# Modulation weights with output columns on partitions, one VectorE multiply-and-sum per tile, and the first projection run behind them block by block of its inner dimension

## The chip, the cores and the metric

One core of one Trainium2 chip runs the kernel. The metric is the device time of one execution in microseconds; the median of three runs of the kernel before is 2373.27 us.

## What is computed

A decoder trunk with two layers, 256 tokens and width 2048, all in float32. Cut to what matters here:

```python
mod = silu(c) @ ada_w[layer] + ada_b[layer]          # c: 2048, ada_w: 2048 x 12288, for each of 2 layers
sh1, sc1, g1, sh2, sc2, g2 = split(mod, 6)           # 2048 each
h = rms_norm(x) * (1 + sc1) + sh1
x = x + g1 * mixer(h)                                # layer 0: MoBA + differential attention, layer 1: sliding window
h = rms_norm(x) * (1 + sc2) + sh2
x = x + g2 * swiglu(h)
out = rms_norm(x) * final_norm
```

The modulation weights are 2 x 2048 x 12288 floats, 192 tiles of 1 MiB, and each is used once, for one row `c`. Nothing of layer 0's first projection can be multiplied with a token before `sc1` and `sh1` are there for the same columns.

## The kernel before

Five programs are written out by hand, one for each engine, and meet on semaphores. SyncE (SP) issues all weight transfers in one fixed order: 1 MiB tiles `raw` (128 partitions x 2048 floats, in a ring of four) for the projections and the FFN, and 1 MiB tiles `ada_raw` (a ring of two) for the modulation. `Phase` (line 62) holds the counts of each stage: `blocks` of 512 output columns, `pairs` of 128-row slices of the inner dimension, and `ada`, the 512-column modulation blocks that are worked off beside it.

Each float32 product is made of three fp32r products. ScalarE copies a weight pair to `w_hi` (`hi`, line 425), VectorE subtracts it from the raw weights to get `w_lo` (`lo`, line 674), four pairs deep, and TensorE runs 12 matmuls of 128x512 on each pair (`pair`, line 1156: lines 1164 to 1166). There are 728 pairs.

**Modulation.** A tile holds inner dimension on partitions and 4 x 512 output columns. `ada_product` (line 694) multiplies a 512-column slice by a per-partition scalar of `cond` and adds it to `acc`: 16 instructions for 512 columns, 4 for each tile, lines 697 and 699. What stands in `acc` is still to be summed over the 128 partitions: TensorE transposes it (`sums`, line 1170: 8 transposes for half a vector, 24 such halves), VectorE reduces the transposed block (`columns`, line 722: line 727), and adds the bias (line 731).

**Start.** `mod0` works off the first eight 512-column blocks (shift and scale of layer 0, 32 tiles). The norm of `x`, its transposes (`norm_blocks`, line 1187), the modulation of the transposed blocks (line 456 on ScalarE, 768 on VectorE) and then the first projection follow.

**First projection.** `ab(0)` to `ab(3)` each make three 512-column blocks (q, k, v of four heads), 24 pairs each, with output column block outermost and inner dimension innermost; in the PE program of `ab(i)` the attention of unit i-1 is interleaved. `ab_rope` (line 803) rotates q and k on VectorE, `ab_v` and `copy_kT` (lines 815, 819) copy on VectorE, and two modulation blocks (8 tiles, 32 products) go beside each `ab(i)`. The output projection (`AB_OUT`, 32 pairs) carries 16 tiles. After it come norm 1 (`to_norm`), the FFN, norm 2, layer 1, norm 3, the second FFN and the last norm.

## Time and profile before

| | |
|---|---|
| median of 3 runs | 2373.27 us (2373.07 to 2379.73) |
| profiled execution, its own time | 2372.14 us |
| its span in the trace | 2370.2 us |
| TensorE busy | 2195.5 us, 93% |
| VectorE busy | 1743.5 us, 74% |
| ScalarE busy | 955.9 us, 40% |
| DMA | 593.12 MB, mean 250 GB/s |

The busy shares are sums over the whole span and say little of a stage; a stage is read from windows cut at the starts of its pairs. TensorE records are pipelined, so that one of 390 ns starts every 227 ns: the distance of the starts is the cost.

### The profile page before, as it was taken

What the parts mean: (1) busy time and instruction counts of PE and PEld (TensorE: products, weight loads), DVE (VectorE), ACT (ScalarE), POOL (GpSimd) and SP (SyncE); (2) the same over time, 40 slices, a digit from 0 to 9 for tenths busy, and PEclk for the clock granted to TensorE, in tenths of its full rate; (3) what the DMA queues carried; (4) which work ended last, traced back from release to release, by engine and by line L of the source; (5) the groups of instructions that cost most, each with busy time, mean ns of one, the idle gap of its engine ahead of it and who ended that gap; (6) DMA issues with size and microseconds to landing.
All of it is one profiled execution on the core that took longest, in us unless ns stands there. A gap on an engine that the chain in (4) does not pass through costs nothing.

```text
span 2370.2 us, 27802 instructions
## 1 busy us (share of the span) xinstructions
PE 2195.5 (93%) x10348; PEld 1831.9 (77%) x10348; DVE 1743.5 (74%) x2089; ACT 955.9 (40%) x1236; POOL 10.2 (0%) x23
## 2 busy tenths in 40 slices
PE   0199999999999999999998999898999999999997
PEld 0178888777888888888886788787888888888886
DVE  6898889998779977798777856498776545455554
ACT  1054434435443344434444344344443344434443
POOL 0000000000000000000000000000000000000000
PEclk9699999999999999999999999899999999999998
DMA  8876776786777977789766633285774555555543
GB/s 337 341 299 271 288 299 234 290 330 256 284 282 296 382 288 289 270 356 357 283 245 252 240 113 111 90 329 214 291 282 176 191 185 194 191 188 191 194 153 149
DMA packets 82437, 593.12 MB, mean 250 GB/s; under 512 B 9408, under 2 KB 9440, under 8 KB 10784
## 3 DMA queue, kind: packets, MB, share of 16 engines
q1 hardware_dynamic: 81056, 587.25, 64.5%
q0 software_dynamic: 1280, 4.51, 0.7%
q8 instruction: 66, 1.08, 0.2%
q14 instruction: 35, 0.29, 0.0%
HBM read 589.62 MB, written 2.10 MB: 250 GB/s over the span
## 4 chain that ended last, share of the span: by engine, by line
PE 49%; issue 35%; DVE 9%; DMA 3%; ACT 1%; DVEq 1%; SPq 0%; POOL 0%; ACTq 0%; POOLq 0%
PE ps L1164 14%; PE ps L1166 14%; PE ps L1165 14%; DVE acc L699 4%; DMA ada_raw<-in_ada 3%; PE ps L1153 2%; DVE w_lo L677 2%; PE ps L1231 1%; PE ps L1236 1%; PE ps L1234 0%; PE ps L1248 0%; PE ps L1251 0%; PE ps L1250 0%; ACT gate L493 0%; DVEq L971 0%
## 5 line engine op out<-in xcount | busy, mean ns | idle before, releaser
L677 DVE TENSOR_TENSOR w_lo<-raw,w_hi 128x1024 fp32r<-128x1024 f32 x728 | 888.7, 1223 | 421.1 <-ACT w_hi L431 417.9
L431 ACT ACTIVATE w_hi<-raw 128x1024 fp32r<-128x1024 f32 x728 | 767.7, 1061 | 1059.4 <-PE ps L1166 958.0
L1164 PE MATMUL ps<-w_hi,xT_hi 128*128 128x512 f32 x1952 | 769.2, 394 | 15.7 <-DVE w_lo L677 7.7
L1166 PE MATMUL ps<-w_hi,xT_lo 128*128 128x512 f32 x1952 | 761.3, 390 | 0.0
L1165 PE MATMUL ps<-w_lo,xT_hi 128*128 128x512 f32 x1952 | 760.3, 390 | 0.0
L699 DVE SCALAR_TENSOR_TENSOR acc<-ada_raw,cond,acc 128x512 f32<-128x512 f32 (+1 forms) x656 | 486.1, 747 | 17.3 <-DMA ada_raw<-in_ada 9.9
L1164 PEld LDWEIGHTS ps<-w_hi,xT_hi 128*128 128x128 f32 x1952 | 367.0, 188 | 93.3 <-issue 14.2
L1166 PEld LDWEIGHTS ps<-w_hi,xT_lo 128*128 128x128 f32 x1952 | 366.7, 188 | 77.4
L1165 PEld LDWEIGHTS ps<-w_lo,xT_hi 128*128 128x128 f32 x1952 | 367.2, 188 | 73.8
L1164 PE MATMUL ps<-w_hi,hT_hi 128*128 128x512 f32 x960 | 377.4, 393 | 3.4 <-DVE hT_lo L896 1.9
L1166 PE MATMUL ps<-w_hi,hT_lo 128*128 128x512 f32 x960 | 374.4, 390 | 0.0
L1165 PE MATMUL ps<-w_lo,hT_hi 128*128 128x512 f32 x960 | 374.2, 390 | 0.0
L1164 PEld LDWEIGHTS ps<-w_hi,hT_hi 128*128 128x128 f32 x960 | 180.7, 188 | 41.8 <-DVE w_lo L677 2.3
L1166 PEld LDWEIGHTS ps<-w_hi,hT_lo 128*128 128x128 f32 x960 | 180.6, 188 | 38.0
L1165 PEld LDWEIGHTS ps<-w_lo,hT_hi 128*128 128x128 f32 x960 | 180.8, 188 | 36.6
L1153 PE MATMUL ps<-ident,work 128*128 128x128 f32 x448 | 71.3, 306 | 47.2 <-ACT work L535 26.3
L1153 PEld LDWEIGHTS ps<-ident,work 128*128 128x128 f32 x448 | 62.9, 161 | 56.3 <-ACT work L535 26.5
L1153 PE MATMUL ps<-ident,acc 128*128 128x128 f32 x192 | 27.3, 296 | 82.7 <-DVE acc L699 82.7
L1153 PEld LDWEIGHTS ps<-ident,acc 128*128 128x128 f32 x192 | 25.0, 154 | 85.3 <-issue 64.5
L1012 DVE TENSOR_TENSOR hT_lo<-ps,hT_hi 128x512 f32 (+1 forms) x44 | 30.4, 692 | 71.3 <-ACT hT_hi L593 71.3
L593 ACT ACTIVATE hT_hi<-ps 128x512 f32 (+1 forms) x44 | 26.4, 599 | 96.4 <-PE ps L1153 96.4
L699 DVE SCALAR_TENSOR_TENSOR acc<-raw,cond,acc 128x512 f32<-128x512 f32 (+1 forms) x64 | 43.1, 746 | 3.1 <-DMA raw<-in_ada 3.0
(145 smaller groups left out, 915.7 us busy)
## 6 DMA issues: line engine op xcount, KB each, us to landing
ada_raw<-in_ada SPq DMA_DIRECT2D x176, 1024.0 KB, 6.2
raw<-in_ffn_in SPq DMA_DIRECT2D x176, 1024.0 KB, 4.8
raw<-in_ffn_out SPq DMA_DIRECT2D x88, 1024.0 KB, 6.6
...
```

The costliest lines, as they stand in the source:

```text
L431: nc.scalar.activation(w_hi[:, p % PAIRS, :, :], raw[:, t % RAW, 2 * (p % 2):2 * (p % 2) + 2, :], ACT.Copy).then_inc(hi_ready, 1)
L593: nc.scalar.activation(hT_hi[:, ds(2 * j, 2), :], bank(4 + b).rearrange("p (k s) -> p k s", k=2), ACT.Copy).then_inc(hTh_done, 1)
L677: tt(w_lo[:, p % PAIRS, :, :], raw[:, (p // 2) % RAW, 2 * (p % 2):2 * (p % 2) + 2, :], w_hi[:, p % PAIRS, :, :].bitcast(F32), ALU.subtract ...
L699: stt(out=dst, in0=src, scalar=cond[:, kt:kt + 1], in1=dst, op0=ALU.mult, op1=ALU.add).then_inc(ada_step, 1)
L1012: tt(hT_lo[:, ds(2 * j, 2), :], bank(4 + b).rearrange("p (k s) -> p k s", k=2), hT_hi[:, ds(2 * j, 2), :].bitcast(F32), ALU.subtract).then ...
L1153: return nc.tensor.transpose(out, in_, ident[:, :])
L1164: mm(out, hi[:, kt, tok], w_hi[:, q % PAIRS, k, :], start=(kt == 0), stop=False)
L1165: mm(out, hi[:, kt, tok], w_lo[:, q % PAIRS, k, :], start=False, stop=False)
L1166: last = mm(out, lo[:, kt, tok], w_hi[:, q % PAIRS, k, :], start=False, stop=(kt == 2 * ph.pairs - 1))
L1231: mm(s0, q(h)[:, 0:P], k(h)[:, 0:P], start=False, stop=True)
L1236: last = mm(ps[:, s1 + P:s1 + SEQ], q(h)[:, P:SEQ], k(h)[:, P:SEQ], start=False, stop=True)
```

## The change

The tiles of the modulation weights are laid out the other way round: a tile is 128 output columns on the partitions and all 2048 inner rows along them. `cond` becomes a row of 2048 on every partition, and one VectorE instruction (`tile`) multiplies a tile by it and writes the sum to one column of `mod`. The products, the partial sums `acc`, the 24 x 8 transposes and the reductions are gone; only the bias is added (`with_bias`). The tiles at the start alternate between scale and shift for the same 128 columns and use four slots (`ada_raw` twice, `spare`, `gate`).

With this, two 128-column slices of the modulated input are known after each four tiles. A new phase `AB0` holds the first unit's three blocks, and in eight rounds each round takes four tiles, the bias, the two slices, and one pair of each of the three blocks, that is, with the inner dimension outermost. Three pairs of banks hold the three sums. The rotations of the first unit follow the eighth round, its transposes stand inside `ab(1)`, and the attention of unit 0 is five pairs later there (`AB_LATER`). The copies of v and of the transposed k move from VectorE to ScalarE; k is rotated into a place of its own (`nat_k`). Each `ab(i)` for i = 1, 2, 3 now carries 12 tiles and `AB_OUT` 12.

```diff
+        self.block0 = prev.block0 + prev.n * prev.evacs if prev else 0
         self.ada0 = prev.ada0 + prev.n * prev.ada if prev else 0
         self.fills = [len(range(s, self.quads, RAW)) for s in range(RAW)]
         self.fills0 = [a + prev.n * b for a, b in zip(prev.fills0, prev.fills)] if prev else [0] * RAW
@@ -83,9 +83,9 @@
...
-
-
-
-FFN_SUMS = (((None, G2[0]), (SH1[1], SC1[1]), (G1[1], None)), ((None, G2[1]), (None, None), (None, None)))
...
+            sp.dma_start(cond[:, :], T["c"].partition_broadcast(P)).then_inc(s_cond, 16)
+            for t in range(TT):
+                sp.dma_start(x[:, t, :], T["x"][:, t, :]).then_inc(x_landed[t], 16)
+            def start_tile(m):
+                if m >= START_SLOTS:
+                    sp.wait_ge(ada_done, ADA_CREDIT + m - START_SLOTS + 1)
+                sp.dma_start(ada_slot[m % START_SLOTS], T["ada"][m]).then_inc(ada_landed[m % START_SLOTS], 16)
+
+            def weights(ph, i, t):
+                sp.wait_ge(lo_ready, LO_CREDIT + 2 * (ph.quad(i, t) - ph.raw_distance(t) + 1))
+                sp.dma_start(raw[:, t % RAW, :, :].rearrange("p a n -> p (a n)"),
+                             T[ph.src][ph.src0 + i * ph.quads + t]).then_inc(raw_landed[t % RAW], 16)
+            for j in range(8):
+                for m in range(4 * j, 4 * j + 4):
+                    start_tile(m)
+                for t in range((3 * j + 1) // 2, (3 * j + 4) // 2):
+                    if t == 3:
+                        sp.wait_ge(s_setup, 1)
+                    weights(AB0, 0, t)
+            for n, ph in enumerate(chain):
...
+            def copy_kT(u):
+                act.wait_ge(kT_done, u + 1)
+                nc.scalar.activation(kT, bank(6, 2).rearrange("p (h s) -> p h s", h=4), ACT.Copy).then_inc(kT_copied, 1)
+
+            def copy_v(u):
+                act.wait_ge(pair_used, AB_IN.used(u - 1, 2) if u else AB_IN.used(-1, 2))
+                nc.scalar.activation(v_ab, bank(2 * (u % 2) if u else 4, 2).rearrange("p (t n) -> p t n", t=TT),
+                                     ACT.Copy).then_inc(v_copied, 1)
...
+            for j in range(8):
+                act.wait_ge(mods_ready, j + 1)
+                act.wait_ge(x0T_done, j + 1)
+                for k in range(2):
+                    kt = 2 * j + k
+                    o = ps[:, (6 + j % 2) * 512 + k * SEQ:(6 + j % 2) * 512 + (k + 1) * SEQ]
+                    last = nc.scalar.activation(o, o, ACT.Identity, bias=mod[:, 0, 0, kt:kt + 1],
+                                                scale=mod[:, 0, 1, kt:kt + 1])
+                last.then_inc(x0m_done, 1)
+                act.wait_ge(x0m_done, j + 1)
+                nc.scalar.activation(xT_hi[:, 2 * j:2 * j + 2, :], bank(6 + j % 2).rearrange("p (k s) -> p k s", k=2),
+                                     ACT.Copy).then_inc(x0h_done, 1)
+                for n in range(3 * j, 3 * j + 3):
+                    hi(AB0, 0, n)
+            copy_v(0)
+            act.wait_ge(s_setup, 1)
+            nc.scalar.activation(lam[:, 2:4], lam[:, 0:2], ACT.Exp).then_inc(lam_exp, 1)
...
+            def tile(slot, q):
+                nc.vector.scalar_tensor_tensor(
+                    out=ada_slot[slot], in0=ada_slot[slot], scalar=1.0, in1=cond[:, :], op0=ALU.mult, op1=ALU.mult,
+                    accum_out=mod_row[:, ds(q, 1)]).then_inc(ada_done, 1)
+
+            def ada(ph, i, a):
+
+                dve.wait_ge(ada_landed[a % ADA_RAW], 16 * ph.ada_fills(i, a))
+                tile(a % ADA_RAW, ph.ada_tile(i, a))
+
+            def start_tile(m):
+
+                dve.wait_ge(ada_landed[m % START_SLOTS], 16 * (m // START_SLOTS + 1))
+                tile(m % START_SLOTS, (1 - m % 2) * KT + m // 2)
 
             def ada_behind(ph, i, p):
 
-                for step in ph.ada_steps(p):
-                    ada(ph, i, step)
...
+            nc.vector.tensor_copy(mask_prev[:, :], masks[:, 128:256])
+            for layer in range(2):
+                scales = ada_bias[:, layer, 1:5:3, :]
+                nc.vector.tensor_scalar(scales, scales, 1.0, None, ALU.add)
+            lv = lam_rows.rearrange("p (a b n) -> p a b n", a=2, b=2)
+            prod = raw[:, 3, 2, 0:256].rearrange("p (a n) -> p a n", a=2)
             tt(prod, lv[:, :, 0, :], lv[:, :, 1, :], ALU.mult)
             dve.drain()
-            nc.vector.tensor_reduce(lam[:, 0:2], prod, AX_X, ALU.add).then_inc(s_setup, 2)
-            dve.wait_ge(s_setup, 5)
-            tt(lam[:, 0:1], lam[:, 3:4], lam[:, 2:3], ALU.subtract)
+            nc.vector.tensor_reduce(lam[:, 0:2], prod, AX_X, ALU.add).then_inc(s_setup, 1)
+            dve.wait_ge(x_landed[1], 16)
+            stt(out=squared[:, 1, :], in0=x[:, 1, :], scalar=1.0, in1=x[:, 1, :], op0=ALU.mult, op1=ALU.mult,
+                accum_out=squares[:, 1, 0:1])
             dve.drain()
-            nc.vector.tensor_scalar(lam[:, 0:1], lam[:, 0:1], -LAMBDA_INIT, None, ALU.add).then_inc(s_setup, 1)
-            repeat(dve, 1, 3, mod0)
-            columns(SH1[0], 0, 6, order=0)
-            columns(SC1[0], 0, 4, order=1)
             norm(0)
-            mod0(3)
-            columns(SH1[0], 1, 6, order=2)
-            columns(SC1[0], 1, 4, order=3)
-            norm_out(0, AB_IN)
+            dve.wait_ge(s_silu_c, 1)
+            for j in range(8):
+                for m in range(4 * j, 4 * j + 4):
+                    start_tile(m)
+                dve.drain()
+                pair_mods = mod[:, 0, 0:2, 2 * j:2 * j + 2]
+                tt(pair_mods, pair_mods, ada_bias[:, 0, 0:2, 2 * j:2 * j + 2], ALU.add).then_inc(mods_ready, 1)
+                lo(AB0, 0, 3 * j)
+                dve.wait_ge(x0h_done, j + 1)
+                tt(xT_lo[:, 2 * j:2 * j + 2, :], bank(6 + j % 2).rearrange("p (k s) -> p k s", k=2),
+                   xT_hi[:, 2 * j:2 * j + 2, :].bitcast(F32), ALU.subtract).then_inc(x0l_done, 1)
+                lo(AB0, 0, 3 * j + 1)
+                lo(AB0, 0, 3 * j + 2)
 
             def ab_stage(stage, u, kind):
 
                 B = kind == "B"
-                if stage == "v":
...
+            ab_rope(0, 0)
+            ab_rope(0, 1)
             ab(1, "A")
...
@@ -1167,20 +1173,9 @@
                                   stop=(kt == 2 * ph.pairs - 1))
                 last.then_inc(pair_used, 1)
 
-            def sums(n, h, b=6, steps=None, read=None):
-
-
-                slot0 = 4 * n % ACC + 2 * h
-                pe.wait_ge(ada_step, ADA_CREDIT + (16 * (4 * n + 2 * h + 2) if steps is None else steps))
-                pe.wait_ge(acc_free, ACC_CREDIT + (4 * n + 2 * h if read is None else read))
-                for c in range(8):
-                    last = tr(ps[:, b * 512 + c * P:b * 512 + (c + 1) * P],
...
+            def first_blocks(j):
+
+                pe.wait_ge(xn_done, j // 2 + 1)
+                if j >= 2:
+                    pe.wait_ge(x0l_done, j - 1)
+                for k in range(2):
+                    kt, at = 2 * j + k, (6 + j % 2) * 512 + k * SEQ
+                    for t in range(TT):
+                        last = tr(ps[:, at + t * P:at + (t + 1) * P], xn[:, t, kt * P:(kt + 1) * P])
+                last.then_inc(x0T_done, 1)
 
             def q_transposes(i):
 
...
-            norm_blocks(0, (2, 3))
+            first_blocks(0)
+            first_blocks(1)
+            for j in range(8):
+                pe.wait_ge(x0l_done, j + 1)
+                for b in range(3):
+                    pair(AB0, 0, b, j, AB0_SLOT[b], xT_hi, xT_lo, q=3 * j + b)
+                if j < 6:
+                    first_blocks(j + 2)
+            pe.wait_ge(s_setup, 1)
 
...
```

**The order on VectorE at the start.** In the program before, behind the loop with the rest of the 32 tiles, this is the last part of the modulation and what stands between it and the first weights (`acc` partial sums, `mod` the vectors, `ps` the banks):

```order
L699 SCALAR_TENSOR_TENSOR acc<-raw,cond,acc 128x512 [waits ada_step,raw_landed3,raw_landed2]
L699 SCALAR_TENSOR_TENSOR acc<-raw,cond,acc 128x512 [waits ada_step] x7
L727 TENSOR_REDUCE mod<-ps 128x8 [waits mods_summed]
L731 SCALAR_TENSOR_TENSOR mod<-mod,ada_bias 128x16
L727 TENSOR_REDUCE mod<-ps 128x8 [waits mods_summed]
L731 SCALAR_TENSOR_TENSOR mod<-mod,ada_bias 128x16
L768 TENSOR_SCALAR ps<-ps,mod 128x256 [waits xT_done]
L768 TENSOR_SCALAR ps<-ps,mod 128x256
L768 TENSOR_SCALAR ps<-ps,mod 128x256 [waits xT_done]
L768 TENSOR_SCALAR ps<-ps,mod 128x256
L773 TENSOR_TENSOR xT_lo<-ps,xT_hi 128x1024 [waits xT_hi_done]
L677 TENSOR_TENSOR w_lo<-raw,w_hi 128x1024 [waits hi_ready] x2
```

And in the changed program, the end of the setup and the first of eight rounds:

```order
L762 RECIPROCAL rstd<-rstd 128x2 [waits root_done]
L722 SCALAR_TENSOR_TENSOR ada_raw,mod<-ada_raw,cond 128x2048 [waits ada_landed0,silu_c_done]
L722 SCALAR_TENSOR_TENSOR ada_raw,mod<-ada_raw,cond 128x2048 [waits ada_landed1]
L722 SCALAR_TENSOR_TENSOR spare,mod<-spare,cond 128x2048 [waits ada_landed2]
L722 SCALAR_TENSOR_TENSOR gate,mod<-gate,cond 128x2048 [waits ada_landed3]
L927 TENSOR_TENSOR mod<-mod,ada_bias 128x2x2
L718 TENSOR_TENSOR w_lo<-raw,w_hi 128x1024 [waits hi_ready]
L930 TENSOR_TENSOR xT_lo<-ps,xT_hi 128x512 [waits first_xT_hi_done]
L718 TENSOR_TENSOR w_lo<-raw,w_hi 128x1024 [waits hi_ready] x2
L722 SCALAR_TENSOR_TENSOR ada_raw,mod<-ada_raw,cond 128x2048 [waits ada_landed0]
```

All products stood ahead of the first `w_lo` before; now four tiles stand ahead of three of them, and the first `w_lo` of a round waits for ScalarE, which follows behind the bias (L927).

**The order on ScalarE at the start.** Before, all blocks of `x` are modulated (`ps`) and copied (`xT_hi`) once, around the first four weight pairs (L431):

```order
L535 ACTIVATE work<-x,rstd 128x512 [waits rstd_done]
L535 ACTIVATE work<-x,rstd 128x512 x7
L456 ACTIVATE ps<-ps,mod 128x256 [waits xT_done,acc_free]
L456 ACTIVATE ps<-ps,mod 128x256
L456 ACTIVATE ps<-ps,mod 128x256 [waits xT_done]
L456 ACTIVATE ps<-ps,mod 128x256
L463 ACTIVATE xT_hi<-ps 128x1024 [waits modulated_dve,modulated_act]
L431 ACTIVATE w_hi<-raw 128x1024 [waits pair_used,raw_landed0]
L431 ACTIVATE w_hi<-raw 128x1024 [waits pair_used]
L456 ACTIVATE ps<-ps,mod 128x256 [waits xT_done]
L456 ACTIVATE ps<-ps,mod 128x256
```

In the changed program the first round and the head of the second:

```order
L553 ACTIVATE work<-x,rstd 128x512 x7
L563 ACTIVATE ps<-ps,mod 128x256 [waits first_xT_done,mods_ready]
L563 ACTIVATE ps<-ps,mod 128x256
L567 ACTIVATE xT_hi<-ps 128x512 [waits first_xT_modulated]
L444 ACTIVATE w_hi<-raw 128x1024 [waits pair_used,raw_landed0]
L444 ACTIVATE w_hi<-raw 128x1024 [waits pair_used]
L444 ACTIVATE w_hi<-raw 128x1024 [waits pair_used,raw_landed1]
L563 ACTIVATE ps<-ps,mod 128x256 [waits first_xT_done,mods_ready]
L563 ACTIVATE ps<-ps,mod 128x256
```

What was one passage of ScalarE is now eight, each behind the bias of its round, and the first `w_hi` of a round stands behind the round's `xT_hi`.

## Rows read from the trace of the kernel before

**Rows 1.** Page, busy time and share of the span by engine

```profile
PE 2195.5 (93%) x10348; PEld 1831.9 (77%) x10348; DVE 1743.5 (74%) x2089; ACT 955.9 (40%) x1236; POOL 10.2 (0%) x23
```

**Rows 2.** Windows by stage: busy us by engine, TensorE clock, DMA share, GB/s

```profile
0.00:126.70 126.70, 14.47 (x65) 13.09 (x65) 95.03 (x151) 19.79 (x39) 4.79 (x13) 0.80 0.85 340
126.70:196.70 70.00, 67.65 (x306) 55.90 (x307) 67.51 (x85) 30.94 (x33) 0.00 (x0) 1.00 0.74 292
196.70:272.40 75.70, 75.70 (x381) 63.75 (x380) 65.30 (x84) 32.42 (x46) 0.00 (x0) 1.00 0.71 278
...
424.90:530.00 105.10, 100.87 (x490) 83.76 (x489) 99.22 (x127) 44.67 (x72) 0.00 (x0) 1.00 0.78 311
...
544.40:1284.00 739.60, 739.20 (x3348) 612.38 (x3348) 604.11 (x684) 305.73 (x324) 0.00 (x0) 1.00 0.77 298
```

**Rows 3.** Timeline, end of the start: start us, us, engine, line, count, idle before

```profile
110.64 5.38 DVE L699 SCALAR_TENSOR_TENSOR acc<-raw,cond,acc 128x512 f32<-128x512 f32 x8
...
116.07 3.67 PE L1153 MATMUL ps<-ident,acc 128*128 128x128 f32 x16 [18.20 <-DVE acc L699]
...
121.08 0.17 DVE L731 SCALAR_TENSOR_TENSOR mod<-mod,ada_bias 128x16 f32<-128x16 f32 x1
...
126.68 0.47 PE L1164 MATMUL ps<-w_hi,xT_hi 128*128 128x512 f32 x1 [1.69 <-DVE w_lo L677]
```

**Rows 4.** Windows of 10 us in the start

```profile
20.00:30.00 10.00, 0.00 (x0) 0.00 (x0) 8.54 (x13) 0.00 (x0) 0.00 (x0) 1.00 1.01 419
110.00:120.00 10.00, 3.67 (x16) 3.27 (x16) 7.63 (x13) 0.00 (x0) 0.00 (x0) 0.50 0.96 387
```

**Rows 5.** Timeline of the start, setup and norm 0

```profile
36.89 0.42 DVE L910 TENSOR_REDUCE lam<-work 128x2 f32<-128x256 f32 x1
...
91.94 0.15 DVE L744 TENSOR_REDUCE ssq<-squares 128x2 f32<-128x8 f32 x1
...
92.61 0.17 DVE L750 RECIPROCAL rstd<-rstd 128x2 f32<-128x2 f32 x1 [0.27 <-ACT rstd L446]
```

**Rows 6.** DMA issues of the start: engine, count, KB, median us to landing

```profile
work<-in_lam POOLq DMA_DIRECT2D x1, 256.0 KB, 13.0
```

**Rows 7.** Groups by line: operands, count | busy us, mean ns | idle before, releasers

```profile
L677 DVE TENSOR_TENSOR w_lo<-raw,w_hi 128x1024 fp32r<-128x1024 f32 x728 | 888.7, 1223 | 421.1 <-ACT w_hi L431 417.9
...
L431 ACT ACTIVATE w_hi<-raw 128x1024 fp32r<-128x1024 f32 x728 | 767.7, 1061 | 1059.4 <-PE ps L1166 958.0 <-DMA raw<-in_ffn_out 47.3 <-DMA raw<-in_swa_in 21.3
...
L699 DVE SCALAR_TENSOR_TENSOR acc<-ada_raw,cond,acc 128x512 f32<-128x512 f32 (+1 forms) x656 | 486.1, 747 | 17.3 <-DMA ada_raw<-in_ada 9.9
...
L456 ACT ACTIVATE ps<-ps,mod 128x256 f32<-128x256 f32 x32 | 16.0, 548 | 36.7 <-DVE mod L731 23.5 <-PE ps L1153 13.2
...
L439 ACT ACTIVATION_READ_ACCUMULATOR xT_lo<-x 128x1 f32 x40 | 7.4, 186 | 0.0
...
L1144 DVE SCALAR_TENSOR_TENSOR work<-x,rstd,gate 128x1024 f32<-128x1024 f32 x4 | 4.9, 1278 | 2.0 <-DMA gate<-in_final_norm 2.0
```

**Rows 8.** Timeline of TensorE in the fourth unit of the first projection

```profile
406.51 1.03 PE L1153 MATMUL ps<-ident,acc 128*128 128x128 f32 x8
407.30 0.48 PE L1164 MATMUL ps<-w_hi,xT_hi 128*128 128x512 f32 x1
...
408.08 0.39 PE L1164 MATMUL ps<-w_hi,xT_hi 128*128 128x512 f32 x1
...
408.76 0.39 PE L1164 MATMUL ps<-w_hi,xT_hi 128*128 128x512 f32 x1
```

**Rows 9.** Timeline of VectorE, one rotation in the second unit

```profile
251.93 0.42 DVE L796 TENSOR_TENSOR gate<-ps,rope_ab 128x256 f32<-128x256 f32 x1
...
256.37 0.75 DVE L699 SCALAR_TENSOR_TENSOR acc<-ada_raw,cond,acc 128x512 f32<-128x512 f32 x1
```

**Rows 10.** Timeline of VectorE and ScalarE in norm 1

```profile
535.94 0.16 DVE L750 RECIPROCAL rstd<-rstd 128x2 f32<-128x2 f32 x1
...
534.67 0.20 ACT L446 ACTIVATE rstd<-ssq 128x2 f32<-128x2 f32 x1 [0.47 <-DVE ssq L746]
```

354 lines of the change are left out of this document (138 added, 216 removed).

## The prediction

> **What bounds the kernel now.** I read the busy times first, then windows by stage, then the timeline at the seams. TensorE is busy for 93% of the span and VectorE for 74% [rows 1]. By stage: nothing of the trunk is multiplied in the first 126.7 us; TensorE's 14.5 us there are transposes. From there each of the four units of the first projection takes 70.0 to 76.8 us with TensorE busy without a gap from the second on [rows 2] (the third has the second's times, the window between them is left out). So the kernel has two parts: a start of 126.7 us on VectorE and DMA, and a rest that TensorE sets. The seam shows the start's chain: last products at 110.6, transposes of `acc` at 116.1, bias at 121.1, first matmul at 126.7 [rows 3]. TensorE's own prices: three matmuls from 408.08 to 408.76, so 0.227 us each and 2.72 for a pair of 12; eight transposes from 406.51 to 407.30, 0.79 us [rows 8].
>
> **The tile.** Eight products of 512 take 5.38 us, 0.67 each [rows 3]. The same kind of instruction, two float32 operands in SBUF and a scalar, has 1278 ns for 1024 elements [rows 7] where one of 512 has 747 (the page's mean for L699), 1.037 ns an element. A tile of 2048 is then 0.67 + 1536 x 1.037 ns = 2.27 us. Its sum output is in no VectorE row. Nearest rows: none (0), or ScalarE's reading of its accumulator, 0.19 us [rows 7]. I take 0.1, nearer to the middle since only a read is added: **2.37 us a tile**, against 4 x 0.67 = 2.7 before.
>
> **A round of the new start**, on VectorE: four tiles 9.5; drain and bias, small operations as in norm 1, 0.35; then it waits for ScalarE, which modulates two slices (2 x 0.55, overlapped: 1.0), copies 512 columns to `xT_hi` (half of `w_hi`'s 1.06, with its fixed part 0.6) and makes the round's first `w_hi` (1.06) [rows 7], 2.75 with the hand-overs; three `w_lo` at 1.14 (starts of one 1223 ns row behind another) and `xT_lo` 0.6: 4.0. Sum **16.6 us**. What lies beside it: transfers of four tiles and one and a half weight tiles, 5.5 MiB = 5.77 MB. At the 419 GB/s of a full stretch [rows 4] that is 13.8 us, hidden; SP refills a tile slot as soon as its tile is summed, 14 us ahead. TensorE has three pairs and four transposes: 8.6 us at full clock, 17.2 at half, since 16 transposes take 3.67 us at the end of the start [rows 3], where the clock is 0.50 [rows 4], against 1.6 at full. It is idle for some 8 us a round, so I expect both levels in each round.
>
> **When the rounds start.** The constants stand first in VectorE's queue: issue at 5.7, landing 13.0 later [rows 6], 18.7. That landing was already beside a full queue of tiles; `cond` as a broadcast row (1 MiB more) and `x` (2 MiB) stand ahead of the tiles now, so that the tiles, not the constants, come later. Casts and lambda, 2 us (L910 was the last of them [rows 5]), the squares of half of `x`, 2.3 as a tile, and the norm, 0.9 [rows 5], follow: first tile at **24.5 us**. The eighth round's last `xT` slice is ready at 24.5 + 7 x 16.6 + 14.4 = 155.1. TensorE's next pair, at half clock, ends at 160.5; the two rotations, 4.4 each [rows 9], and the first `w_lo` of unit 1 follow in VectorE's queue: 170.6. TensorE has finished its three pairs by about 167 and waits. I add 2.0 for a clock that fell in the gap: unit 1 begins at **172.6**, against 196.7 before: **-24.1**.
>
> **Behind the start.** Unit 1 also has the transposes of q and k of unit 0: 2 x 0.79, **+1.6**. VectorE's load in a unit: 65.3 [rows 2], less 32 products (21.1) and two copies (2.3), plus 12 tiles (28.4): 70.3 of TensorE's 75.7. I tallied both queues pair by pair: VectorE stays one to nine us ahead, least behind the second rotation. In unit 1 the two late rotations make 79.5 against 77.3, but the attention comes five pairs later. I put **0** for stalls; the cover is a lead of only 1 us at one place, and its loss is a rival below. ScalarE takes the copies, at 32.4 of 75.7 [rows 2]. The partial sums' transposes: 24 halves, four in the start, six in the three norms, where TensorE waits for VectorE anyway, and 14 in full stretches: 14 x 0.79 = **-11.1**. In norm 1 the reduction started at 534.55 and the reciprocal at 535.94, while ScalarE's root was ready at 534.87 [rows 10]: 0.85 goes; in the other two norms the root comes 1.3 later behind a table load, 0.2 each: **-1.2**. The output projection has 105.1 - 100.9 = 4.2 us of gaps with VectorE busy for 99.2 [rows 2]; 64 products (42.7) become 12 tiles (28.4): I take half the gaps, **-2.0**. Its bounds are 0 and 4.2. In the FFN nothing waits for products: 0, covered by 135 us of idle VectorE in the first one's 740. Bytes are the same.
>
> Sum: -24.1 + 1.6 - 11.1 - 1.2 - 2.0 = **-36.8 us**. From the profiled execution's 2372.1 that gives 2335.3; its own time is 1.1 under the median, from which I count: 2373.3 - 36.8 = **2336.5**.
>
> **Rule against row.** The products L699 read two float32 tensors from SBUF at 1.037 ns an element and write one, with no sum output. The Trainium skill (Vector Engine (DVE) Microarchitecture Reference, "Points that are easy to get wrong") says of this instruction that with two non-bf16 SBUF sources it runs at half throughput, because no read port is left for the accumulator. The rows contradict it for the form without a sum, and no run here shows the form with one. By the rule the kernel would be the first rival.
>
> **Rivals.**
> - *The sum halves the tile's rate*: 2048 x 1.037 = 2.1 us more a tile, 4.4 in all. For: the accumulator is new here. Against: the same operands stream at full rate. The rounds take 25.1 us and unit 1 begins 68 us later, +44 against before; each unit's VectorE load is 95 to 104 where TensorE needs 76, together +66; the output projection +4, the first FFN (84 tiles, VectorE from 604 to 747 of 740) +20. With the -12 of transposes and norms: **2495**, slower. It decides from 0.7 us more a tile: 32 x 0.7 = 22 in the rounds, 3 x (12 x 0.7 - 4.7) = 11 in the units, which uses up the gain. 10%.
> - *VectorE binds in the units*: its 5 us of slack are not where the two rotations stand, and TensorE waits 3 to 4 us in each of three. For: the lead of 1 us. Against: the tally. **2347**. 17%.
> - *TensorE stays at half clock through the rounds*: 17.2 > 16.6 sets the round, +5, and the tail of three pairs and the head of unit 1 cost 5 more. For: 0.50 in the start and 8 us idle a round. Against: bursts of three pairs are longer than the transposes that stayed cold [rows 3]. **2346**. 12%. The Trainium skill (TensorE: Matmul & The Clock Gate, "Loop structure matters more than you think") warns of this loop nest, a wait in front of every K step; by it the clock falls in every round.
> - *Transfers set the round*: 5.77 MB at the start's mean 340 GB/s [rows 2] is 17.0; at the 3.35 us a tile of the old start (32 tiles in 107 us) it is 18.4, +14: **2351**. Against: there the slots were refilled in groups, here singly. 8%.
> - *The start gains nothing*, since constants, norm and rotations only move: only the transposes and norms remain, **2361**. The order speaks against it. 3%.
>
> **Numbers.** Forecast 50%, 2336.5. Its own bounds: no cost of the sum (-3), clock never late (-5), all gaps (-2) give 2326; a sum of 0.19 (+3) and 3 us of stalls 2343. With the second to fourth rivals the range is 2324 to 2358, which leaves out the first and the last and a little more. A difference under 0.3% (7 us) can't be told from none here: faster 0.88, same 0.02, slower 0.10.
>
> **What would show it.** Right: tiles near 2.4 us, 16.6 us from a round's first tile to the next's, first tile at 24 to 25, unit 1 beginning near 172, units of 75 to 77 us, no TensorE gaps in them above 1 us. Wrong: tiles above 3 us; VectorE idle before tiles for DMA; TensorE waiting for `w_lo` in units 1 to 3.

## The result and the profile after

The changed kernel takes **2331.45 us** (median of 4 runs, 2328.86 to 2332.46) against 2374.66 us for the kernel before (4 runs, 2373.07 to 2379.73): ratio **0.9818, 95% interval 0.9805 to 0.9832**. The forecast was 2336.5, -36.8 us; the measured difference is -43.2. The profiled spans are 2329.6 and 2370.2 us, -40.6, and the account below is made between these two.

A "pair" is 12 matmuls of one pair of weight slices, as before. Its lines are now L1170 to L1172, `w_hi` is L444, `w_lo` L718, the tile L722, the bias L927.

The times of the table, and those of pairs below, lie up to 0.3 us behind the start of the matmul's own row in the timeline (unit 1: 163.5 here, 163.24 there), in all kernels alike.

| first matmul of | before | after | difference | gained in the stage |
|---|---|---|---|---|
| unit 1 | 196.7 | 163.5 | -33.2 | -33.2 |
| unit 2 | 272.4 | 245.3 | -27.1 | +6.1 |
| unit 3 | 348.1 | 321.0 | -27.1 | 0.0 |
| output projection | 424.9 | 400.1 | -24.8 | +2.3 |
| first feed-forward | 544.4 | 517.9 | -26.5 | -1.8 |
| end of span | 2370.2 | 2329.6 | -40.6 | -14.1 |

Page of the kernel after, busy time and share of the span by engine, to be held against [rows 1]: VectorE has 120 us less to do, TensorE 4 us less.

```profile
PE 2191.1 (94%) x10156; PEld 1821.1 (78%) x10156; DVE 1623.3 (70%) x1676; ACT 964.1 (41%) x1247; POOL 9.9 (0%) x22
```

Windows by stage, kernel after (window, length, then busy us of PE, PEld, DVE, ACT, POOL, TensorE clock, DMA share, GB/s), against [rows 2]: the start, units 1 to 3, the output projection, the first feed-forward layer.

```profile
0.00:163.50 163.50, 89.86 (x321) 70.78 (x322) 118.91 (x135) 52.77 (x74) 4.57 (x12) 0.88 0.87 341
...
163.50:245.30 81.80, 80.65 (x398) 67.45 (x397) 72.08 (x79) 34.05 (x49) 0.00 (x0) 0.96 0.77 298
245.30:321.00 75.70, 75.70 (x381) 63.72 (x380) 66.52 (x72) 30.75 (x44) 0.00 (x0) 1.00 0.83 322
321.00:400.10 79.10, 75.43 (x363) 62.43 (x362) 68.06 (x87) 34.74 (x56) 0.00 (x0) 1.00 0.82 324
400.10:504.60 104.50, 100.36 (x474) 83.21 (x472) 82.82 (x87) 48.00 (x75) 0.00 (x0) 0.98 0.75 301
517.90:1250.00 732.10, 732.10 (x3288) 606.34 (x3286) 561.24 (x507) 308.38 (x326) 0.00 (x0) 1.00 0.78 304
```

Timeline of VectorE, kernel after, one round of the start (start us, us, engine, line, operation, tiles, count, idle before).

```profile
71.22 2.28 DVE L722 SCALAR_TENSOR_TENSOR ada_raw<-ada_raw,cond 128x2048 f32<-128x2048 f32 x1
73.44 0.08 DVE L722 DVE_READ_ACCUMULATOR ada_raw<-ada_raw,cond 128x1 f32 x1
73.44 2.28 DVE L722 SCALAR_TENSOR_TENSOR ada_raw<-ada_raw,cond 128x2048 f32<-128x2048 f32 x1
...
80.25 0.16 DVE L927 TENSOR_TENSOR mod<-mod,ada_bias 128x4 f32<-128x4 f32 x1
83.04 1.23 DVE L718 TENSOR_TENSOR w_lo<-raw,w_hi 128x1024 fp32r<-128x1024 f32 x1 [2.63 <-ACT w_hi L444]
84.19 0.68 DVE L930 TENSOR_TENSOR xT_lo<-ps,xT_hi 128x512 fp32r<-128x512 f32 x1
84.79 2.35 DVE L718 TENSOR_TENSOR w_lo<-raw,w_hi 128x1024 fp32r<-128x1024 f32 x2
87.06 2.28 DVE L722 SCALAR_TENSOR_TENSOR ada_raw<-ada_raw,cond 128x2048 f32<-128x2048 f32 x1
```

Three things are to be seen. A tile starts every 2.21 us, and the reading of its sum (0.08 us) starts with the next tile and lies beside it: it costs nothing of its own. The round from tile to tile is 87.06 - 71.22 = **15.84 us**. And 2.63 us of it VectorE is idle for `w_hi`. The round three later, on ScalarE, says why: ScalarE stood idle 11.37 us for the bias, and its three `w_hi` come only then, behind the modulation and `xT_hi`.

```profile
127.94 0.99 ACT L563 ACTIVATE ps<-ps,mod 128x256 f32<-128x256 f32 x2 [11.37 <-DVE mod L927]
128.96 0.60 ACT L567 ACTIVATE xT_hi<-ps 128x512 fp32r<-128x512 f32 x1
129.45 2.94 ACT L444 ACTIVATE w_hi<-raw 128x1024 fp32r<-128x1024 f32 x3
```

Timeline of VectorE at the end of the start, kernel after: the last bias and slice, the first instructions of the two rotations, the first `w_lo` of unit 1.

```profile
143.57 0.17 DVE L927 TENSOR_TENSOR mod<-mod,ada_bias 128x4 f32<-128x4 f32 x1
...
147.51 0.68 DVE L930 TENSOR_TENSOR xT_lo<-ps,xT_hi 128x512 fp32r<-128x512 f32 x1
...
152.89 0.42 DVE L805 TENSOR_TENSOR gate<-ps,rope_ab 128x256 f32<-128x256 f32 x1 [2.43 <-PE ps L1172]
...
157.34 0.42 DVE L805 TENSOR_TENSOR gate<-ps,rope_ab 128x256 f32<-128x256 f32 x1
...
161.87 2.36 DVE L718 TENSOR_TENSOR w_lo<-raw,w_hi 128x1024 fp32r<-128x1024 f32 x2 [0.21 <-ACT w_hi L444]
```

Three places where TensorE waited, at the head of unit 1 and in unit 3 (timeline of TensorE, kernel after): the first is that `w_lo` behind the rotations; the other two were not forecast.

```profile
163.24 0.76 PE L1170 MATMUL ps<-w_hi,xT_hi 128*128 128x512 f32 x1 [4.93 <-DVE w_lo L718]
```

```profile
340.21 0.87 PE L1159 MATMUL ps<-ident,gate 128*128 128x128 f32 x6 [2.04 <-DVE gate L863]
364.44 1.09 PE L1159 MATMUL ps<-ident,work 128*128 128x128 f32 x8 [1.63 <-DVE work L885]
```

The waits in unit 3, kernel after: ScalarE's for weights, and the transfer queue's, 321 to 400 us (engine and line, what it waited for, us in total, times, longest).

```profile
ACT w_hi L444 <- DMA raw<-in_ab_in: 23.7, 7, 5.0
```

```profile
SPq L362 <- DVE ada_raw L722: 63.1, 12, 12.7
```

**Where the last 14.1 us are.** I compared the distances of all 728 pairs' first matmuls, kernel by kernel. Behind the first feed-forward matmul, exactly ten pairs come 0.79 or 0.80 us sooner behind the one ahead, at 698.3, 706.9, 800.3, 819.8, 966.9, 975.5, 1065.3, 1084.8, 1761.4 and 1770.1 us: the ten halves of transposes that stood there, 7.9 us. Two seams behind norms give 0.5 and 0.6. The pairs about norm 2 (1266 to 1303 us) give 3.5 net, the first of them 2.8. The last 1.6 us are steps below 0.3 us each.

### The profile page after: what moved, and what is told of

The parts are those of the page before. It is cut to its first block, busy times and chain, and to the rows that moved or that the text cites. A ratio compares the mean times of both kernels' runs of the same rounds, so it can differ in the third digit from the quotient of the medians.

```text
span 2329.6 us, 26534 instructions
## 1 busy us (share of the span) xinstructions
PE 2191.1 (94%) x10156; PEld 1821.1 (78%) x10156; DVE 1623.3 (70%) x1676; ACT 964.1 (41%) x1247; POOL 9.9 (0%) x22
## 4 chain that ended last, share of the span: by engine, by line
PE 51%; issue 35%; DVE 9%; ACT 3%; DMA 2%; DVEq 1%; POOL 0%; SPq 0%; ACTq 0%; POOLq 0%
PE ps L1170 15%; PE ps L1172 15%; PE ps L1171 15%; DVE w_lo L718 3%; DVE ada_raw L722 2%; PE ps L1159 2%; ACT w_hi L444 1%; DVE spare L722 1%; DVE gate L722 1%; ACT gate L512 1%; DMA raw<-in_lam 1%; DMA raw<-in_swa_in 1%; PE ps L1227 0%; PE ps L1232 0%; PE ps L1180 0%
## 5 line engine op out<-in xcount | busy, mean ns | idle before, releaser
L718 DVE TENSOR_TENSOR w_lo<-raw,w_hi 128x1024 fp32r<-128x1024 f32 x728 | 882.9, 1223 | 518.5 <-ACT w_hi L444 513.8
L444 ACT ACTIVATE w_hi<-raw 128x1024 fp32r<-128x1024 f32 x728 | 766.0, 1061 | 1003.6 <-PE ps L1172 866.9
L1170 PE MATMUL ps<-w_hi,xT_hi 128*128 128x512 f32 x1952 | 778.7, 399 | 57.8 <-DVE xT_lo L930 43.6
L1172 PE MATMUL ps<-w_hi,xT_lo 128*128 128x512 f32 x1952 | 768.8, 394 | 0.0
L1171 PE MATMUL ps<-w_lo,xT_hi 128*128 128x512 f32 x1952 | 768.7, 394 | 0.0
L1170 PEld LDWEIGHTS ps<-w_hi,xT_hi 128*128 128x128 f32 x1952 | 372.1, 191 | 138.4 <-DVE xT_lo L930 45.9
L1172 PEld LDWEIGHTS ps<-w_hi,xT_lo 128*128 128x128 f32 x1952 | 371.7, 190 | 79.8
L1171 PEld LDWEIGHTS ps<-w_lo,xT_hi 128*128 128x128 f32 x1952 | 372.6, 191 | 75.6
L722 DVE SCALAR_TENSOR_TENSOR ada_raw<-ada_raw,cond 128x2048 f32<-128x2048 f32 x176 | 401.1, 2283 | 2.9 <-DMA ada_raw<-in_ada 1.9
L1170 PE MATMUL ps<-w_hi,hT_hi 128*128 128x512 f32 x960 | 376.4, 392 | 2.1 <-DVE hT_lo L899 1.9
L1172 PE MATMUL ps<-w_hi,hT_lo 128*128 128x512 f32 x960 | 374.2, 390 | 0.0
L1170 PEld LDWEIGHTS ps<-w_hi,hT_hi 128*128 128x128 f32 x960 | 180.8, 188 | 39.7 <-DVE hT_lo L899 2.2
L1172 PEld LDWEIGHTS ps<-w_hi,hT_lo 128*128 128x128 f32 x960 | 180.6, 188 | 38.0
L1159 PEld LDWEIGHTS ps<-ident,work 128*128 128x128 f32 x448 | 59.7, 154 | 58.5 <-issue 40.6
L563 ACT ACTIVATE ps<-ps,mod 128x256 f32<-128x256 f32 x16 | 7.9, 533 | 84.0 <-DVE mod L927 84.0
L980 DVE TENSOR_TENSOR work<-ps,gate 128x1024 f32<-128x1024 f32 x28 | 34.1, 1219 | 12.3 <-PE ps L1172 11.7
L983 DVE TENSOR_TENSOR x<-x,work 128x1024 f32<-128x1024 f32 x32 | 39.2, 1225 | 2.4
```

The source lines that it names most:

```text
L444: nc.scalar.activation(w_hi[:, p % PAIRS, :, :], raw[:, t % RAW, 2 * (p % 2):2 * (p % 2) + 2, :], ACT.Copy).then_inc(hi_ready, 1)
L718: tt(w_lo[:, p % PAIRS, :, :], raw[:, (p // 2) % RAW, 2 * (p % 2):2 * (p % 2) + 2, :], w_hi[:, p % PAIRS, :, :].bitcast(F32), ALU.subtract ...
L722: nc.vector.scalar_tensor_tensor(out=ada_slot[slot], in0=ada_slot[slot], scalar=1.0, in1=cond[:, :], op0=ALU.mult, op1=ALU.mult, accum_out ...
L980: tt(upd, src, gate[:, ds(j * NT, NT)].unsqueeze(1).broadcast_to([P, TT, NT]), ALU.mult)
L983: tt(xs, xs, upd, ALU.add).then_inc(evacuated, 1)
L1159: return nc.tensor.transpose(out, in_, ident[:, :])
```

## The experiments

All are edits of the changed kernel. Each ran beside the kernel before; the ratio is to that one. The changed kernel itself is at 0.9818 (0.9805 to 0.9832), 2331.45 us.

**1. The tiles ahead of the rounds.** All 32 tiles first, then the eight rounds. In the transfer queue the first four blocks of weights go behind the fifth to eighth group of four tiles, the other eight behind all tiles.

```
-            for j in range(8):
-                for m in range(4 * j, 4 * j + 4):
-                    start_tile(m)
+            for m in range(START_TILES):
+                start_tile(m)
+            for j in range(8):
                 dve.drain()
```

> All 32 multiplies of the start come ahead of the eight rounds; the rounds' products, k-outermost, are unchanged. If the gain of the start is the overlap of products with tiles (the prediction's own account), the tiles end at about 32 x 2.5 = 80 us behind 21, at about 103 us, since the transfers alone set them there, and 24 pairs at 2.72 us, the slices of xT and the rotations follow: unit 1 begins at about 174 us instead of 163.5, and the time is about 2342 us, some 11 us over the changed kernel. If the gain of the start is merely that sums and transposes left TensorE, the order is worth nothing: 2331 us.

Measured: **2358.75 us**, ratio 0.9936 (0.9917 to 0.9955); unit 1 begins at 189.6. The windows of its start, up to its first pair and from there:

```profile
0.00:114.00 114.00, 2.16 (x9) 1.79 (x10) 79.50 (x81) 16.68 (x26) 4.59 (x12) 1.00 0.91 368
114.00:189.60 75.60, 70.68 (x313) 57.98 (x314) 42.27 (x55) 37.78 (x48) 0.00 (x0) 0.98 0.50 181
```

The overlap of products with tiles is worth 27 us, much more than the 11 I expected: the tiles took 2.67 us each, held by their transfers (first bias at 109.1 instead of 103), and the rounds, bound by TensorE, 8.65 us each (pair distances 3.08, 2.84, 2.72) where I had put 8.16, without the round's four transposes. So of the 33 us the start gained, 26 are the order; only 7 remain if the same work stands in the old order (189.6 against 196.7).

**2. The first `w_hi` of each round ahead of the modulation.**

```
             for j in range(8):
+                hi(AB0, 0, 3 * j)
                 act.wait_ge(mods_ready, j + 1)
...
-                for n in range(3 * j, 3 * j + 3):
+                for n in range(3 * j + 1, 3 * j + 3):
```

> ScalarE makes the first w_hi of a round before it waits for that round's modulation. If the VectorE chain sets the round (four tiles, three w_lo, one xT_lo, and 2.63 us in which VectorE waits for this very w_hi), the period falls from 15.83 us by up to 2.6 us until the transfers bind at 5.77 MB / 419 GB/s = 13.8 us: 8 x 2.0 = 16 us less, about 2315 us. If the transfers or TensorE set the round already, the period stays at 15.8 us and the time at 2331 us.

Measured: **2315.86 us**, ratio 0.9754 (0.9735 to 0.9772), 15.6 us less. The round in VectorE's timeline has lost the wait:

```profile
103.54 0.16 DVE L928 TENSOR_TENSOR mod<-mod,ada_bias 128x4 f32<-128x4 f32 x1
103.62 1.22 DVE L719 TENSOR_TENSOR w_lo<-raw,w_hi 128x1024 fp32r<-128x1024 f32 x1
105.39 0.69 DVE L931 TENSOR_TENSOR xT_lo<-ps,xT_hi 128x512 fp32r<-128x512 f32 x1 [0.55 <-ACT xT_hi L568]
```

The distance from round to round falls from 15.83 to 14.1 us in all rounds, since VectorE's 2.63 us of waiting have become 0.80 (0.55 for `xT_hi`, 0.25 for `w_hi`), and unit 1 begins 13.9 us sooner, at 149.6; the rest lies behind. The transfers run at 402 GB/s with a share of 0.98, and TensorE's clock is 0.88 (window 36 to 135 us): VectorE's chain did set the rounds of the changed kernel, neither the transfers nor TensorE.

```profile
36.00:135.00 99.00, 73.57 (x278) 58.22 (x278) 92.70 (x92) 31.65 (x43) 0.00 (x0) 0.88 0.98 402
```

At 14.1 us it is still VectorE's chain: from 50 to 135 us VectorE waits for ScalarE only (3.3 and 1.8 us in all), never for a tile to land. With a share of 0.98 the transfers leave little room behind it; how much wasn't tried.

**3. Halves of unit 1 ahead of the second rotation.**

```
             ab_rope(0, 0)
+            lo(AB_IN, 0, 0)
+            lo(AB_IN, 0, 1)
             ab_rope(0, 1)
```

and the same on ScalarE, ahead of the copy of v.

> The halves of the first two pairs of unit 1 are made ahead of the second rotation and of the copy of v, instead of behind them. If TensorE waits there for w_lo behind the rotation (w_lo 161.87, rotation 157.34 to 161.8), unit 1 begins about 4.3 us earlier, and TensorE, less cold, loses less at its head; some of it is given back if the transposes of k then wait for the second rotation: 2326 to 2328 us. If the start is set by what is behind (transfers of unit 1), the time stays at 2331 us.

Measured: **2329.49 us**, ratio 0.981 (0.9791 to 0.9828). Unit 1 begins 4.8 us sooner, at 158.7, but then TensorE waits for the third pair's `w_lo`:

```profile
158.44 0.47 PE L1176 MATMUL ps<-w_hi,xT_hi 128*128 128x512 f32 x1 [0.40 <-DVE w_lo L721]
167.28 0.50 PE L1176 MATMUL ps<-w_hi,xT_hi 128*128 128x512 f32 x1 [2.24 <-DVE w_lo L721]
```

and the half clock comes behind it (0.67 over the next 5.2 us). The first feed-forward matmul is 4.3 us sooner (513.6), yet the median falls by 2 only, which the interval doesn't separate from nothing. In the trace 3.4 us are lost again at two pairs of layer 1's attention, which is experiment 8's matter.

**4. TensorE kept at work in the rounds.** A product with a matrix of zeros is added to an open sum 18 times behind rounds 0 to 6.

```
+                    for _ in range(FILL):
+                        mm(bank(2)[:, 0:P], zeros[:, :], ident[:, :], start=False, stop=False)
```

> TensorE adds a zero product to an open sum 18 times behind rounds 0 to 6, in the time in which it would idle; numbers don't change. If the pairs that ran at half clock (4.44 us instead of 2.72 in the last round, 5.26 us at the head of unit 1) cost the end of the start, the time falls by 1.7 to 4 us, to about 2328 us. If the half clock only lengthened pairs that had time to spare, it stays at 2331 us; and if the filler delays the slices of xT, it rises by up to 0.5 us a round, to 2335 us.

Measured: **2328.73 us**, ratio 0.9808 (0.979 to 0.9826). Windows from 38 to 150 us, the changed kernel and this one:

```profile
38.00:150.00 112.00, 78.79 (x281) 62.05 (x280) 92.91 (x93) 30.97 (x42) 0.00 (x0) 0.84 0.91 360
```

```profile
38.00:150.00 112.00, 98.60 (x534) 84.58 (x534) 92.92 (x93) 30.96 (x42) 0.00 (x0) 0.95 0.91 359
```

The clock rises from 0.84 to 0.95 (the first pair of a round, 4.4 to 5.3 us in all eight rounds before, takes 2.9 in three of them) and the rounds stay at 15.83 us: the half clock had time to spare there. Unit 1 begins at 163.6. The 2.7 us of the medians aren't separated from nothing by the intervals; in the trace 1.0 lies at the first pair of unit 1 (4.21 instead of 5.26 us), 0.7 in unit 3 and 1.6 net at two pairs of the output projection.

The last round is another matter, and this experiment doesn't reach it, although zero products stand ahead of it: its first pair takes 4.44 us in both kernels, and the first rotation, whose sum that pair completes, waits for it. In the combinations of experiment 9 that pair takes 2.9 us. VectorE's wait for it, here and in the last combination:

```profile
153.00 0.42 DVE L807 TENSOR_TENSOR gate<-ps,rope_ab 128x256 f32<-128x256 f32 x1 [2.43 <-PE ps L1175]
```

```profile
137.24 0.42 DVE L824 TENSOR_TENSOR gate<-ps,rope_ab 128x256 f32<-128x256 f32 x1 [0.54 <-PE ps L1195]
```

In experiment 2, whose rounds are as short as the combination's, the wait is 2.04: the half clock costs the end of the start about 1.5 us, and nothing in the rounds before.

**5. A slower tile.**

```
             def tile(slot, q):
+                part = ada_slot[slot][:, 0:640]
+                tt(part, part, part, ALU.max)
+                dve.drain()
```

> Every tile of modulation weights gets a second VectorE instruction of 640 columns (the maximum of a piece with itself, nothing changes) and a drain, some 0.75 us a tile. If VectorE's tiles set the start as said, it lengthens by 32 x 0.75 = 24 us; in the units 12 x 0.75 = 9 us go on VectorE's 66.5 to 72 us of 76 to 82 us, so 0 to 5 us a unit: some 2331 + 24 + 0 to 15 = 2355 to 2370 us, which is the rival of a slow summing tile at the point where it was said to decide (2361 to 2370). If the transfers or TensorE set the start, 2331 to 2340 us.

Measured: **2391.38 us**, ratio 1.0072 (1.0054 to 1.0089): 60 us over the changed kernel, and slower than the kernel before. The added instruction takes 818 ns, with its drain 0.9 us a tile. Units 2 and 3:

```profile
276.60:358.50 81.90, 77.81 (x382) 64.69 (x381) 78.47 (x87) 32.21 (x47) 0.00 (x0) 0.98 0.81 314
358.50:445.00 86.50, 78.91 (x364) 64.98 (x363) 78.04 (x98) 34.23 (x56) 0.00 (x0) 0.96 0.75 291
```

The start lengthened by 29.2 us (32 x 0.91), the units by 2.1, 6.2 and 7.4, the output projection by 1.0. The rest, behind the first feed-forward matmul, took 14.5 us more, where I expected none: 8.7 of them are in five pairs in the middle of the first feed-forward layer, where TensorE waited for `w_lo`, two of them here.

```profile
801.43 0.50 PE L1173 MATMUL ps<-w_hi,hT_hi 128*128 128x512 f32 x1 [0.71 <-DVE w_lo L718]
825.40 0.50 PE L1173 MATMUL ps<-w_hi,hT_hi 128*128 128x512 f32 x1 [1.87 <-DVE w_lo L718]
```

VectorE's idle time there is an average; these waits suggest that its lead is short where a tile, the copies of a hidden block and a `w_lo` stand together.

**6. Ten groups of eight transposes back** in the feed-forward layers, at their old places.

```
+                            if (layer, s) in ((0, 0), (0, 1), (1, 0)) and p in (0, 3):
+                                eight()
```

and the same two in the input blocks of the other groups.

> The ten groups of eight transposes that the change removed from the feed-forward stretches stand again at their ten places, of the identity into a bank that nobody reads. If TensorE sets those stretches, each costs the 0.79 us by which the pair behind it moved: 7.9 us, 2339.3 us. If something else set them, under 2 us.

Measured: **2342.66 us**, ratio 0.9851 (0.9826 to 0.9877). The ten pairs come 0.78 to 0.81 us later, each, as expected. The time is 11.2 us up and not 7.9: in the profiled run another 2.6 us are at two pairs of layer 1's attention (at 1487 and 1492 us), which the edit doesn't touch. One of the four runs took 2333.38 us, at a mean clock of 0.980 where the other three had 0.977. The reading rests on the ten distances, not on the time.

**7. Tiles asked for later.** In the three units the transfer queue asks for each tile two blocks of weights later.

```
+                            late += [(ph, i, a) for a in ph.ada_after(t)]
+                            while len(late) > LAG:
+                                ada(*late.pop(0))
```

> In the three units the transfer queue asks for each tile of modulation weights two blocks of projection weights later than now, so that a wait for a free tile buffer (63.1 us in 12 waits in unit 3) holds up the weights less. If that order makes the weights late in unit 3 (ScalarE waits 4.95 and 4.19 us for them, TensorE 2.2 us), the 2.2 us and perhaps some of the norm's start come back: 2327 to 2329 us. If the bandwidth is the limit (0.82 busy), 2331 us; if now VectorE waits for its tiles, up to 2335 us.

Measured: **2330.94 us**, ratio 0.9814 (0.9797 to 0.983): nothing in the time. But unit 3 falls from 79.1 to 77.0 us, and ScalarE's wait for this unit's weights, 23.7 us in 7 places, is gone. (Unit 1 falls from 81.8 to 80.4, at its first two pairs, 4.26 us for 5.26 and 3.51 for 3.91, as in experiment 4: that is the clock.) The queue's waits in unit 3 are now split between tiles and weights:

```profile
SPq L363 <- DVE ada_raw L734: 41.2, 11, 8.6
SPq L372 <- DVE w_lo L730: 24.1, 8, 8.3
```

Of the two gaps in unit 3, the one at 340.2 us (2.04) is gone: it came from the order of the queue. With two buffers for tiles and four for weights, a tile that waits for its buffer holds up weights that have theirs. The gap at 364.4 (1.63) stands as it was, though ScalarE no longer waits for weights ahead of it:

```profile
361.73 1.09 PE L1171 MATMUL ps<-ident,work 128*128 128x128 f32 x8 [1.64 <-DVE work L897]
```

It is VectorE's: a rotation, a tile of 2.2 us in one piece and a `w_lo` stand directly ahead of that stage of the attention (353.99 to 361.79 us in the changed kernel), where the kernel before had two products, 1.5 us, in the tile's place. With the longer tile of experiment 5 this pair takes 7.79 us, with the changed kernel's 5.36, before 3.51. That the one-piece tile makes the gap is read from these rows; a tile in pieces wasn't tried. The first feed-forward matmul is 2.6 us sooner, and those are lost again at the same two pairs at 1487 us (+2.4 and +0.7).

**8. TensorE kept at work in the last attention units of layer 1.** In experiments 1, 3, 6, 7 and in the first of the combinations, those two pairs came between 4.4 us sooner and 3.4 us later, with the same code there (in 2, 4 and 5 within 0.1 us). Windows of the changed kernel:

```profile
1460.00:1470.00 10.00, 7.69 (x52) 6.71 (x53) 2.42 (x6) 4.87 (x19) 0.00 (x0) 0.83 0.01 2
1470.00:1480.00 10.00, 6.51 (x43) 5.22 (x42) 5.30 (x14) 4.90 (x20) 0.00 (x0) 0.83 0.00 1
1480.00:1490.00 10.00, 9.15 (x35) 8.31 (x36) 2.61 (x4) 1.54 (x2) 1.06 (x2) 0.50 0.16 48
```

The edit:

```
+                    if stage in ("pT01", "yT") and g >= 37:
+                        for _ in range(14 if stage == "pT01" else 6):
+                            mm(bank(0)[:, 0:P], zeros[:, :], ident[:, :], start=False, stop=False)
```

> The changed kernel with zero products (14 and 6 at a time) added to an open sum in the waits of the last units of the sliding-window attention, where the granted clock was 0.83, 0.83 and 0.50 in three stretches of 10 us behind 1460 us, and where the pairs behind came by up to 4.4 us earlier or 3.4 us later in one kernel than in another whose code there is the same. If the clock makes these differences, the time falls by 3 to 6 us, to 2325 to 2328 us, and its runs lie closer together; if the waits for VectorE and ScalarE set the stretch, it stays at 2331 us.

Measured: **2327.47 us** (5 runs, 2327.03 to 2329.99), ratio 0.981 (0.9795 to 0.9824). The same windows:

```profile
1460.00:1470.00 10.00, 9.75 (x89) 9.28 (x87) 2.18 (x5) 4.25 (x16) 0.00 (x0) 1.00 0.01 2
1470.00:1480.00 10.00, 9.27 (x81) 8.70 (x80) 5.19 (x14) 4.90 (x20) 0.00 (x0) 1.00 0.01 2
1480.00:1490.00 10.00, 9.78 (x64) 8.90 (x65) 4.01 (x6) 2.61 (x3) 1.07 (x2) 1.00 0.38 140
```

The clock stays at its upper level and the two pairs come 3.2 us sooner in all. The interval overlaps that of the changed kernel, and the runs lie hardly closer together (3.0 us for 3.6); the pairs and the clock show the effect, the time alone doesn't. In the first of the combinations, where the pairs come soonest, the clock is 1.00 over the last 10 us of the stretch instead of 0.50. So this stretch takes a time that depends on when the clock falls in it, and a gain of 2 to 4 us made upstream can be lost or doubled here. That is why experiments 3 and 7 move less than their own stages, and probably why the runs of experiment 6 lie apart (the one run at 2333.38 has no profile). It isn't the only such stretch: eight pairs of the output projection, from 408.9 us in the changed kernel, take 32.2 us there and 30.5 in experiments 3 and 4, with the same code and the clock's fall at another moment.

**9. Combinations.** Experiments 2, 3 (with four pairs and the transposes of k two pairs later) and 4 together:

> Three edits together: the first w_hi of each round ahead of the modulation, the halves of four pairs (instead of two) ahead of the second rotation with the transposes of k two pairs later, and TensorE kept at work between the rounds. If the gains measured alone are independent (15.6, 2.0 and 2.7 us), 2311 us; with the transposes of k later a further 2 to 3 us of the seam come back, 2308 us. If the filler now delays the shorter rounds, 2313 to 2316 us.

Measured: **2316.19 us** (2311.71 to 2318.56), ratio 0.9756 (0.9739 to 0.9773), level with experiment 2 alone. That is the number of the third case, but not its reason: the rounds take 14.1 us as in experiment 2. In the profiled run, the lowest of the four, unit 1 begins at 143.2 (163.5 in the changed kernel), but its fourth and fifth pairs take 5.1 us each, behind the late rotation, and its twelfth 2.8 us more than in the changed kernel; unit 2 begins at 230.6, only 0.4 us ahead of experiment 2's. The wait behind the late rotation was moved, not removed.

With the later tiles of experiment 7 added:

> The three edits together (2316.2 us, profiled 2309.8) and the later tiles in the units. If the 2.8 us that the later tiles gave up to the feed-forward layer (they were lost again behind 1441 us, where the clock fell) come through, 2313 us; if they only move a wait, 2316 us.

Measured: **2314.54 us** (5 runs, 2313.41 to 2316.11), ratio 0.9753 (0.9739 to 0.9767). In its profile the first feed-forward matmul comes 3.5 us sooner than without the later tiles, but behind 1441 us the two pairs of experiment 8 come 3.8 us later than in the changed kernel, where the profile without the later tiles had them 4.4 us sooner. And with the zero products of experiment 8:

> The same with the zero products in the waits of the last attention units. If the clock there is what made the three edits' runs spread from 2311.7 to 2318.6 us, this one lies at or under the lowest of them less the 2.8 us, at 2305 to 2310 us, its runs within 2 us; if not, at 2313 us as the kernel without them.

Measured: **2310.28 us** (5 runs, 2308.39 to 2314.01), ratio **0.9733** (0.9719 to 0.9747): 64 us under the kernel before and 21 under the changed one. The clock in its rounds is 1.00 (window 35 to 134 us) at the same 14.1 us a round:

```profile
35.00:134.00 99.00, 91.27 (x528) 79.31 (x528) 92.71 (x92) 31.67 (x43) 0.00 (x0) 1.00 0.98 401
```

Most of the 21 us are experiment 2's; its interval and this one's overlap. The runs did not come to lie within 2 us. The profiled one is the highest of the five, and in it the clock fell at the end of the same stretch in spite of the zero products; the two pairs come 4.9 us later behind the pair ahead of them than in experiment 8:

```profile
1463.00:1473.00 10.00, 9.30 (x48) 8.89 (x48) 2.02 (x5) 1.75 (x3) 1.06 (x2) 0.66 0.06 8
```

The other four ran 3.0 to 5.6 us faster, at a mean clock of 0.988 to 0.991 instead of 0.987. They have no profile, so that the clock in this stretch is what spreads the runs is likely and not shown.

## Why the prediction was right, and where it was off

The direction, the mechanism of the start and the likeliest case were right, and the time lies 5 us under the forecast, in the range. That it lies so near is in part luck. By stages of the trace, the start was 9.1 us and everything behind the first feed-forward matmul 5.8 us better than forecast; unit 1 was 4.5, unit 3 3.9 and the output projection 2.6 us worse. These cancel to 3.9. By its own steps:

- **The tile**, forecast 2.37 us: 2.21 from start to start. The 0.1 for the sum was too much, it lies under the next tile, and 1536 x 1.037 ns was a little high.
- **The round**, forecast 16.6: 15.84. Four tiles at 2.21 are 0.65 less; VectorE's wait for the modulation and `w_hi`, 2.75 forecast, is 2.63. That transfers and TensorE were hidden is shown by experiment 2: an order that cuts VectorE's wait by 1.8 us cuts the round by 1.73, and unit 1 begins 13.9 us sooner.
- **Where the rounds start**: 24.5 forecast (its terms, 18.7, 2, 2.3 and 0.9, add up to 23.9), 23.72 in the trace. Last `xT` slice at 148.2 for 155.1: 0.8 from the first tile, 5.4 from seven rounds, 0.7 in the last one.
- **Begin of unit 1**: 172.6 forecast, 163.5: those 6.9, and from the slice to the unit 15.3 instead of 17.5. The 2.0 us for a fallen clock were due one pair later: the first pair of unit 1 took 5.26 us instead of 2.72. The half clock that the prediction put on the last round's first pair was there: 4.44 us. The start's -24.1 was thus -33.2, of which the clock gave back 2.5 in unit 1. Experiment 1 shows that 26 of the 33 are the overlap on which the sum was built.
- **Stalls in the units, forecast 0**: this is the step that failed. Unit 1 took 6.1 us more, where 1.6 was forecast for the transposes; 2.5 are the clock, 1.2 a gap at 205.4 us in which TensorE waits for VectorE (L869). Unit 3 took 2.3 more where two halves (-1.6) should have made it shorter: 3.9 off, in two gaps. The prediction looked for stalls in VectorE's tally. For the first gap (2.1 us) experiment 7 shows that it is the transfer queue, where a tile in front waits for its buffer; the prediction said of that queue only that slots are refilled at once, which holds for the start's four slots and not for the units' two. The second (1.8 us) is VectorE's, behind a rotation, as the second rival had it, but at 1.8 us here and 1.2 in unit 1 instead of 3 to 4 in each of three units; the tally had missed it.
- **Fourteen halves, -11.1**: ten (-7.9) show at 0.79 each, and experiment 6 puts each back. The four in unit 3 and the output projection can't be told from the gaps there.
- **Norms -1.2**: norms 1 and 3 gave 0.5 and 0.6 at their seams. About norm 2 3.5 us went, unforecast. The weights behind it landed sooner: ScalarE's first `w_hi` of them starts 2.2 us behind the last pair ahead of the norm in the kernel before and 0.6 us ahead of that pair now, and in VectorE's queue the norm stands behind the `w_lo` made from it. That was read from the trace alone and not tried.
- **Output projection -2.0**, with norm 1 and its two halves -4.4: the stage gave 1.8. The gaps did not close: eight pairs in its middle (408.9 to 441.1 us), beside the last unit's attention, take 32.2 us where the kernel before took 29.4, of which 1.7 hang on the moment at which the clock falls (experiment 8). VectorE has two whole tiles among its work there; whether they hold up TensorE wasn't tried.
- **Feed-forward 0**: right for this tile. Experiment 5 shows that the cover was thinner than the 135 us of idle VectorE said: 0.9 us more a tile cost 14.5 us behind that point.

Of the rivals, the halved rate fell with the first tile: 2048 elements in 2.21 us are 1.08 ns each, with the sum. The rule of the Trainium skill (Vector Engine (DVE) Microarchitecture Reference, "Points that are easy to get wrong") that two non-bf16 SBUF sources halve the throughput for want of a port for the accumulator disagrees with this trace; the measurement decides. The rival's break-even, given as 0.7 us a tile, was about right for a partly wrong reason: 0.9 us cost 59.9, so the 43.2 gained are used up at about 0.65 (an estimate in proportion); a quarter of the cost came from behind the first projections, where the break-even had counted nothing. The half clock did occur in every round (the first pair of each took 4.4 to 5.3 us instead of 2.72, and the clock was 0.84 from 38 to 150 us). The Trainium skill (TensorE: Matmul & The Clock Gate, "HAM oscillation — how this bites in real kernels") has the same for a loop that waits for a transfer in front of each K step; here the wait is for VectorE. (The section that the prediction named shows the wait in front of each output tile.) Experiment 4 shows that it costs nothing in the rounds, since VectorE set them; at the last round's end it costs about 1.5 us, and at the head of unit 1 2.5. The transfers did not set the round, though at 14.1 us they nearly do.
